# The context gate g2 moves into the expert loop, and the next mixer adds two accumulators

## The chip, the cores and the metric

The kernel runs on one core of a Trainium2 chip. The metric is the device time of one execution in microseconds (us). Before the change it was 2565.54 us, the median of three runs (2559.32 to 2566.08). The engines are TensorE (PE, matmuls; PEld is its weight load), VectorE (DVE), ScalarE (ACT), GpSimd (POOL) and the sync engine (SP), which only issues DMAs. All data are float32 unless a row says otherwise.

## The reference, cut to what matters

The program is a two-layer backbone over 512 latent tokens and 256 context tokens of width 1024. Layer 0 has a mixer of RG-LRU and differential attention and then a mixture of experts (MoE) over all 768 tokens. Layer 1 has an S5 mixer and then an MoE over the 512 latent tokens. The MoE routes each token to 6 of 64 experts (hidden width 256) and adds a shared expert; its result is multiplied by the modulation row g2 (g2c for context tokens) and added to x.

```python
def moe_ffn(h, ...):
    affinity = sigmoid(h @ router_w)
    _, idx = lax.top_k(affinity + router_bias, TOP_K)
    s_sel = take_along_axis(affinity, idx, -1)
    gates = s_sel / sum(s_sel) * ROUTED_SCALE
    ...                                   # tokens sorted by expert, in blocks
    def expert_block(acc, blk):
        tok, g, e = blk
        y = swiglu(h_ext[tok], w_gate[e], w_up[e], w_down[e])
        return acc.at[tok].add(y * g[:, None]), None
    ...
    return acc[:n_tok] + swiglu(h, ws_gate, ws_up, ws_down)

# layer 0
out = moe_ffn(concatenate([h2c, h2]), *moe_w)
ctx = ctx + g2c * out[:n_ctx_tok]
x = x + g2 * out[n_ctx_tok:]
# layer 1: the S5 mixer reads rms_norm(x) and rms_norm(ctx), then
x = x + g1 * y
x = x + g2 * moe_ffn(h2, *moe_w)
```

## The kernel before

`moe_blocks` (L681) runs once per layer. Ahead of its loop stand the norm, the router, the shared expert (TensorE L1360 into a PSUM bank, ScalarE L1054 into `ysh`, DMA L1056 by ScalarE's queue into the first accumulator in DRAM, `accs[0]`, tile by tile) and a table of items. An item is an expert with up to 128 tokens (wide) or up to 64 (narrow). This input has 34 wide and 38 narrow items in layer 0, and 16 wide and 50 narrow in layer 1.

The loop (`trips`, L815 to L825) walks a written order: in trip b each engine does its steps of wide item i, then of narrow item i, each step behind a branch that asks whether the item is there. So 34 trips of layer 0 and 16 of layer 1 have both items (paired trips), the others a narrow item alone. The order of one engine's steps is fixed; engines meet only at semaphores. In a trip,
- SP loads the next items' gate, up and down weights (1 MB each, L855 and L861) into a ring of two slots for wide items and three for narrow ones;
- GpSimd gathers the tokens of a later item (L946, L952) and scatters a result with add into DRAM: wide items into `accs[0]` (L963), narrow ones into `accs[1]` (L974, two rows of 512 per token);
- TensorE multiplies by gate and up (L1431 wide, L1442 narrow), transposes the hidden rows (L1471 narrow), multiplies by down (L1460 wide, L1481 narrow), and in between turns one-hot marks into token indices and gates (L1369) and transposes gathered tokens (L1376, L1382);
- VectorE does `gated_wide`, `gated_narrow`, `rest_wide` and `rest_narrow`. `rest_wide` reads off indices and gate of a later wide item (`tokens`, L1238 to L1246) and makes the marks of the one behind it (`mark_wide`, L1224). `rest_narrow` first copies the transposed hidden rows from PSUM (L1283), for which TensorE's L1481 waits, and then does the same for a narrow item (`mark_narrow`, L1231);
- ScalarE does the silu, the evictions of transposed tokens (L1014, L1018) and the eviction of the result, scaled by the gate: L1085 for a wide item, L1092 for a narrow one.

At the end SP loads the g2 rows (L902) and both accumulators (L905), VectorE adds the two, multiplies by g2 and adds x (L1296, L1298, L1300, 128x1024 each, per tile of 128 tokens), and SP stores x tile by tile (L909), in layer 0 to a DRAM buffer `x_mid`, in layer 1 to the output.

`s5_mixer` (L1934) follows layer 0. SP loads x_mid in four pieces of 96 partitions x 2048 (L2005) into `XS`. ScalarE squares each of its eight rows (L2082), VectorE waits for small vectors, prepares them and the state's powers (L2142 to L2162) and scales the rows (L2165). Later SP loads x a second time, in the layout of the residual, from x_mid (L2032), while GpSimd loads `Tb` (L2071) for TensorE (L2314).

## Time and profile before

| | |
|---|---|
| median of three runs | 2565.54 us |
| profiled execution: its own time, its span | 2561.44 us, 2559.7 us |
| TensorE busy, share of the span | 2148.3 us, 84% |
| VectorE busy | 908.9 us, 36% |
| ScalarE busy | 607.8 us, 24% |
| GpSimd busy | 453.5 us, 18% |
| DMA over the span | 672.72 MB, mean 263 GB/s |

The span is what the trace covers of the profiled execution. A row of a timeline gives start, duration, engine, line, operation, output<-inputs and shape, and in brackets the engine's idle time ahead of it with what ended it; "issue" there means that the profile shows nothing that was waited for. A row of a group gives total busy time, the mean of one in ns, and the idle time ahead of all of them. Layer 0's expert loop runs from about 711 to 1453 us, the S5 mixer from about 1492 to 1812, layer 1's loop from about 1897 to 2528.

### The profile page before, as it was taken

The numbers are of one execution on the slowest core, as the hardware profiler recorded it, in microseconds if no ns is written. First come the engines' busy times: TensorE is split into PE (matmuls) and PEld (weight loads), VectorE is DVE, ScalarE is ACT, GpSimd is POOL, SyncE is SP. The second block draws the span as 40 slices with busy tenths as digits, with TensorE's granted clock in tenths as the row PEclk, the third lists the DMA queues.
The fourth block names the chain that finished last, engine by engine and source line by source line (L and its number), as shares of the span: only waits on it lengthen the run. The fifth ranks groups of instructions, "written<-read, shape, count | busy, mean of one in ns | idle before, by whom it ended". The sixth has DMA issues, their size and how long they took to land. (4 is left out here: it accounts for less than half of the span.)

```text
span 2559.7 us, 39554 instructions
## 1 busy us (share of the span) xinstructions
PE 2148.3 (84%) x11733; PEld 1190.5 (47%) x11734; DVE 908.9 (36%) x2012; ACT 607.8 (24%) x1047; POOL 453.5 (18%) x423
## 2 busy tenths in 40 slices
PE   5889999896999999999999516489789999987873
PEld 3665445644444444444444315154444444444442
DVE  8854375824512121111111267922431111111113
ACT  3443243602122121121212113130222122211110
POOL 1000000002112222222222211200113222232321
PEclk8999999998999999999999858799899999999997
DMA  9971102005699999999998557960389999899995
GB/s 354 374 266 38 36 30 82 1 0 194 263 334 359 352 358 359 354 358 350 356 364 286 178 181 245 272 224 0 144 353 380 353 358 358 277 388 365 392 379 196
DMA packets 167668, 672.72 MB, mean 263 GB/s; under 512 B 37858, under 2 KB 40898, under 8 KB 123546
## 3 DMA queue, kind: packets, MB, share of 16 engines
q1 hardware_dynamic: 116650, 577.23, 58.8%
q0 software_dynamic: 38208, 69.04, 11.1%
q10 hardware_dynamic: 12720, 25.27, 2.6%
q8 instruction: 54, 0.88, 0.1%
q14 instruction: 36, 0.29, 0.0%
HBM read 622.28 MB, written 89.24 MB: 278 GB/s over the span
## 5 line engine op out<-in xcount | busy, mean ns | idle before, releaser
L1431 PE MATMUL banks_l<-slotw_l,xTw_l 128*128 128x512 f32 x800 | 357.9, 600 | 24.8 <-issue 24.8
L1442 PE MATMUL banks_l<-slotn_l,xTn_l 128*64 128x256 f32 x2816 | 326.5, 385 | 35.1 <-issue 35.1
L1442 PEld LDWEIGHTS banks_l<-slotn_l,xTn_l 128*64 128x64 f32 x2816 | 212.1, 138 | 180.9 <-issue 107.8
L1431 PEld LDWEIGHTS banks_l<-slotw_l,xTw_l 128*128 128x128 f32 x800 | 148.5, 191 | 236.1 <-issue 236.1
L1481 PE MATMUL banks_l<-slotn_l,late_l 128*64 128x512 f32 x704 | 189.9, 615 | 18.2 <-DVE late_l L1283 16.3
L1460 PE MATMUL banks_l<-slotw_l,late_l 128*128 128x512 f32 x400 | 191.8, 602 | 15.4 <-DVE late_l L1269 15.4
L946 POOL DMA_INDIRECT xgw_l<-moe_h,idxw_l x58 | 60.7, 1047 | 770.9 <-PE banks_l L1376 634.5
L974 POOL DMA_INDIRECT moe_acc<-late_l,idxn_l x88 | 141.1, 1603 | 200.8 <-DMA moe_acc<-late_l,idxn_l 183.4
L1266 DVE TENSOR_TENSOR late_l<-late_l,banks_l 128x256 f32<-128x256 f32 x50 | 21.1, 422 | 341.0 <-ACT late_l L1072 341.0
L1231 DVE TENSOR_TENSOR onehotn_l<-iota_slot_l,rank_l 128x512 bf16 (+1 forms) x98 | 79.3, 809 | 133.5 <-issue 133.5
L556 PE MATMUL ps_a<-W_a,hT_a 128*128 128x512 f32 x288 | 124.1, 592 | 0.0
L952 POOL DMA_INDIRECT xgn_l<-moe_h,idxn_l x96 | 102.0, 1063 | 89.3 <-DVE idxn_l L1243 56.2
L2359 PE MATMUL ps_s<-UV_s,ZU_s 128*128 128x512 f32 x256 | 110.1, 592 | 0.7 <-ACT ZU_s L2106 0.7
L1092 ACT ACTIVATE late_l<-banks_l,gslotn_l 128x512 f32<-128x512 f32 x88 | 60.5, 688 | 184.7 <-PE banks_l L1481 171.3
L916 POOL MEMSET ident_l<- 128x128 f32 x2 | 0.4, 205 | 583.5 <-POOLq L69 428.6
L1072 ACT ACTIVATE late_l<-banks_l 128x256 f32<-128x256 f32 x50 | 19.2, 384 | 350.1 <-PE banks_l L1431 340.9
L1460 PEld LDWEIGHTS banks_l<-slotw_l,late_l 128*128 128x128 f32 x400 | 68.5, 191 | 71.3 <-issue 71.3
L1014 ACT ACTIVATE xTw_l<-banks_l 128x512 f32<-128x512 f32 x108 | 64.5, 597 | 151.8 <-PE banks_l L1376 149.8
L1077 ACT ACTIVATE late_l<-banks_l 128x128 f32<-128x128 f32 x88 | 24.5, 278 | 310.1 <-PE banks_l L1442 306.0
L963 POOL DMA_INDIRECT moe_acc<-yw_l,idxw_l x50 | 79.5, 1589 | 97.1 <-ACT yw_l L1085 95.9
L556 PEld LDWEIGHTS ps_a<-W_a,hT_a 128*128 128x128 f32 x288 | 54.7, 190 | 67.7 <-issue 67.4
L510 PE MATMUL ps_a<-hT_a,W_a 128*128 128x512 f32 (+1 forms) x256 | 83.0, 486 | 1.0 <-ACT hT_a L195 1.0
(397 smaller groups left out, 3057.0 us busy)
## 6 DMA issues: line engine op xcount, KB each, us to landing
slotn_l<-in_exp_w_gate SPq DMA_DIRECT2D x88, 1024.0 KB
slotn_l<-in_exp_w_up SPq DMA_DIRECT2D x88, 1024.0 KB
slotn_l<-in_exp_w_down SPq DMA_DIRECT2D x88, 1024.0 KB
slotw_l<-in_exp_w_gate SPq DMA_DIRECT2D x50, 1024.0 KB
slotw_l<-in_exp_w_up SPq DMA_DIRECT2D x50, 1024.0 KB
slotw_l<-in_exp_w_down SPq DMA_DIRECT2D x50, 1024.0 KB
w_p<-in_mod_w SPq DMA_DIRECT2D x12, 2048.0 KB, 15.7
...
```

The costliest lines, as they stand in the source:

```text
L510: last = pe.matmul(bank(4 + 2 * (f % 2), b - a, a), W[:, c % 2, k, f * P:(f + 1) * P], hT[:, k, a:b], start=(k == 0), stop=(k == KD - 1))
L556: last = pe.matmul(bank(n % 4), hT[:, k, t * P:(t + 1) * P], W[:, c % 2, k, :], start=(k == 0), stop=(k == KD - 1))
L952: pool.indirect_dma_start(xg_n[b % 3][:], None, h_half, bass.IndirectOffsetOnAxis(idx[1][b][:].bitcast(U32), 0), bounds_check=last_half, o ...
L963: pool.indirect_dma_start(accs[0], bass.IndirectOffsetOnAxis(idx[0][b][:].bitcast(U32), 0), y_w[b % 2][:], None, bounds_check=last_row, oo ...
L974: pool.indirect_dma_start(acc_half, bass.IndirectOffsetOnAxis(idx[1][b][:].bitcast(U32), 0), y_n[b % 2], None, bounds_check=last_half, oob ...
L1014: act.activation(xT_w[b % 2][:, 4 * half:4 * half + 4, :], pT_w.rearrange("p (k c) -> p k c", c=P), ACT.Copy).then_inc(W['xT_done'], 1)
L1231: dve.tensor_tensor(onehot[1][:].rearrange("p t (a s) -> p t a s", a=2), where, rank[:, :, bass.ds(e, 1)].rearrange("p t (a o) -> p t a o" ...
L1431: last = pe.matmul(pGU_w, xT_w[b % 2][:, k, :], wgu[0][b % WIDE_RING][:, :, k, :], start=(k == 0), stop=(k == KD - 1))
L1442: last = pe.matmul(pGU_n[H * side:H * side + H, b % 2], xT_n[b % 2][:, k % 4, H * (k // 4):H * (k // 4) + H], w[:, :, k, P * side:P * side ...
L1460: last = pe.matmul(pY_w[:, half * 512:(half + 1) * 512], hidT_w[:, k, :], wd[0][b % WIDE_RING][:, k, half * 512:(half + 1) * 512], start=( ...
L1481: last = pe.matmul(pY_n[H * side:H * side + H, :], hidT_n[:, H * k:H * k + H], w[:, k, side * 512:(side + 1) * 512], start=(k == 0), stop= ...
L2359: last = pe.matmul(ps[:, (2 * (u % 4) + half) * 512:(2 * (u % 4) + half + 1) * 512], zT[:, k, m * P:(m + 1) * P], glu[n][:, k, half, :], s ...
```

## The change

The accumulators start otherwise. `accs[1]` gets x in place of zeros (SP, L858), and `accs[0]` gets the shared result multiplied by g2: VectorE's `start_row` (L1264) multiplies one tile of `ysh` into the buffer of x, and ScalarE's queue stores it (`store_start`, L1060). In the loop a result is multiplied by gate and g2 as it leaves PSUM, on VectorE and no longer on ScalarE (`result_wide`, L1324; the end of `rest_narrow`, L1332). In layer 0 an item can hold latent and context tokens, so g2 differs by row: for each item VectorE first makes the row's g2 in the result buffer as `g2_dif * late_row + g2_lat` (L1316 for a wide item), with `late_row` 1 or 0 per token (L1256). VectorE has six steps in a trip where it had four. The final multiply by g2 and add of x are gone. In layer 1 one add per tile is left; in layer 0 nothing is loaded or stored, and the S5 mixer loads both accumulators (L2066), adds them row by row (L2201) and copies the residual out of SBUF (L2077).

```diff
@@ SP, start of moe_blocks
+            for s in range(streams):
+                sp.dma_start(g2[:, s, :], mr[s:s + 1, 5 * D:6 * D].to_broadcast([P, D])).then_inc(R['g2_in'], 16)
             for t in range(NT):
-                sp.dma_start(accs[1][t * P:(t + 1) * P, :], zero).then_inc(R['zero_out'], 16)
+                sp.dma_start(accs[1][t * P:(t + 1) * P, :], x[:, t, :]).then_inc(R['x_kept'], 16)
@@ SP, end of moe_blocks: the g2 loads go; the acc loads and the stores stay only for the output
+            if 'x_out' in st:
                 for t in range(NT):
                     for k, dst in enumerate((acc, acc1)):
                         sp.dma_start(dst[:, t, :], accs[k][t * P:(t + 1) * P, :]).then_inc(acc_in[t], 16)
@@ ScalarE, shared expert, tile t
-                act.dma_start(accs[0][t * P:(t + 1) * P, :], ysh[t % 2][:]).then_inc(y_out[t % 2], 16)
+                if t:
+                    store_start(t - 1)          # waits for start_row(t - 1)
@@ ScalarE, rest_wide (rest_narrow alike)
-                act.wait_ge(W['y_mm'], i + 1 + WIDE_RING)
-                act.wait_ge(yw_added, i * 16 + 16)
-                act.activation(y_w[b % 2][:], pY_w, ACT.Copy, scale=gslot[0][b][:]).then_inc(W['y_done'], 1)
@@ VectorE, tokens
+                if streams > 1:
+                    dve.tensor_scalar(late_row[kind][b][:], idf[kind][:], float(LAT - BIG), None, ALU.is_ge)
@@ VectorE, ahead of the loop
+            def start_row(t):
+                s = 1 if t >= NT - ctx_tiles else 0
+                dve.wait_ge(R['sh_y_done'], 2 * t + 2)
+                dve.tensor_tensor(x[:, t, :], ysh[t % 2][:], g2[:, s, :], ALU.mult).then_inc(R['init'], 1)
@@ VectorE, the loop
                 mark_wide(i + (AHEAD + 1))
+                if streams > 1:
+                    dve.scalar_tensor_tensor(out=y_w[b % 2][:], in0=g2_dif, scalar=late_row[0][b][:], in1=g2_lat,
+                                             op0=ALU.mult, op1=ALU.add).then_inc(W['g_done'], 1)
-            def rest_narrow(i, q, b):
+            def turned_narrow(i, q, b):
                 dve.wait_ge(N['hidT_mm'], i + 1)
                 dve.wait_ge(N['y_mm'], i + NARROW_RING)
                 dve.tensor_copy(hidT_n, pHT[:, 0, :]).then_inc(N['hidT_done'], 1)
+            def result_wide(i, q, b):
+                dve.wait_ge(W['y_mm'], i + 1 + WIDE_RING)
+                dve.scalar_tensor_tensor(out=y_w[b % 2][:], in0=pY_w, scalar=gslot[0][b][:],
+                                         in1=y_w[b % 2][:] if streams > 1 else g2_lat,
+                                         op0=ALU.mult, op1=ALU.mult).then_inc(W['y_done'], 1)
+            def rest_narrow(i, q, b):
                 tokens(1, i + AHEAD, (b + AHEAD) % UNROLL)
                 mark_narrow(i + (AHEAD + 1))
+                ...                             # the g2 row of the item (layer 0), then its result, 128x512 each
@@ S5 mixer: SP, VectorE
+                for part, dst in zip(parts, (X, X1)):
+                    sp.dma_start(dst[:, 2 * j:2 * j + 2, :], part...[:, 2 * j:2 * j + 2, :]).then_inc(x_in[j], 16)
+            for s in range(SL):
+                dve.wait_ge(x_in[s // 2], 32)
+                dve.tensor_tensor(X[:, s, :], X[:, s, :], X1[:, s, :], ALU.add).then_inc(S['x_sum'], 1)
-                                 xin[0:LAT]...[2 * m + hh]).then_inc(S['xres_in'], 16)      # SP L2032
+                            sp.dma_start(x[hh * 64:hh * 64 + 64, m, :], X[0:64, 2 * m + hh, :]).then_inc(S['xres_in'], 16)
```

Smaller parts: 32 one-column memsets at the head of each MoE on VectorE; in layer 0 VectorE makes `g2_lat` and `g2_dif` once ahead of the loop, and SP's first narrow down load waits for it; in the S5 mixer, SP's and GpSimd's steps for the modulation bias wait for the copied residual.

How the rows of the program move is shown at three places. First VectorE in layer 0's loop, between the indices of a wide item and the narrow item's indices, in one trip. Before:

```order
L1224 ISA
L1224 TENSOR_TENSOR onehotw_l0<-iota_slot_l0,rank_l0 128x768
L821 UNCONDITIONAL_BRANCH
L821 COMPARE_AND_BRANCH
L1281 REGISTER_ALU
L1282 REGISTER_ALU
L1283 COPY late_l0<-banks_l0 128x128
L1284 ISA
L1237 REGISTER_ALU
L1238 TENSOR_REDUCE gslotn4_l0<-banks_l0 128x1
L1239 TENSOR_REDUCE idfn_l0<-banks_l0 128x1
```

After:

```order
L1237 TENSOR_TENSOR onehotw_l0<-iota_slot_l0,rank_l0 128x768
L1316 SCALAR_TENSOR_TENSOR yw0_l0<-x,lroww0_l0 128x1024
L828 UNCONDITIONAL_BRANCH
L828 COMPARE_AND_BRANCH
L1320 REGISTER_ALU
L1321 REGISTER_ALU
L1322 COPY late_l0<-banks_l0 128x128
L828 UNCONDITIONAL_BRANCH
L828 COMPARE_AND_BRANCH
L1325 REGISTER_ALU
L1327 REGISTER_ALU
L1328 SCALAR_TENSOR_TENSOR yw0_l0<-banks_l0,gslotw0_l0,yw0_l0 128x1024
```

Behind the mark (L1224, now L1237) stands the making of the g2 row (L1316), and only then the copy of the narrow item's hidden rows (L1283, now L1322); the wide result (L1328) follows it.

Second the sync engine, from the last weight load of layer 0 to the S5 mixer's small loads. Before (of the twelve L905 rows the last three):

```order
L905 DMA slotw1_l0<-moe_acc1 128x1024
L905 DMA slotw0_l0<-moe_acc0 128x1024
L905 DMA slotw1_l0<-moe_acc1 128x1024
L909 DMA x_mid<-x 128x1024 x6
L699 UNCONDITIONAL_BRANCH
L2002 UNCONDITIONAL_BRANCH
L2005 DMA XS_s<-x_mid 96x2048 x4
L2008 DMA vec_s<-modrow 64x2x16 x2
L2009 DMA vec_s<-in_norm1_g 64x16
L2010 DMA lam_s<-s5_l8 128x256
```

After:

```order
L699 UNCONDITIONAL_BRANCH
L2062 UNCONDITIONAL_BRANCH
L2066 DMA XS_s<-moe_acc0 96x2048
L2066 DMA ZU_s<-moe_acc1 96x2048
L2066 DMA XS_s<-moe_acc0 96x2048
L2066 DMA ZU_s<-moe_acc1 96x2048
L2066 DMA XS_s<-moe_acc0 96x2048
L2066 DMA ZU_s<-moe_acc1 96x2048
L2066 DMA XS_s<-moe_acc0 96x2048
L2066 DMA ZU_s<-moe_acc1 96x2048
L2069 DMA vec_s<-modrow 64x2x16 x2
L2070 DMA vec_s<-in_norm1_g 64x16
```

The loads of x_mid come right behind the loop as loads of both accumulators, to the mixer's own tiles; the loads, the stores and the g2 rows between are gone.

Third ScalarE at the head of layer 1's loop: L1054 (now L1073) evicts a tile of the shared expert, L1056 (now L1062) stores one, L1014 and L1018 (now L1029 and L1033) evict transposed tokens. Before:

```order
L1043 ACTIVATE late_l1<-banks_l1 128x256
L1054 ACTIVATE yw0_l1<-banks_l1 128x512 x2
L1056 DMA moe_acc0<-yw0_l1 128x1024
L1014 ACTIVATE xTw_l1<-banks_l1 128x512
L1054 ACTIVATE yw1_l1<-banks_l1 128x512 x2
L1056 DMA moe_acc0<-yw1_l1 128x1024
L1014 ACTIVATE xTw_l1<-banks_l1 128x512
L1018 ACTIVATE xTn_l1<-banks_l1 128x512
L1014 ACTIVATE xTw_l1<-banks_l1 128x512
```

After:

```order
L1073 ACTIVATE yw0_l1<-banks_l1 128x512 x2
L1062 DMA moe_acc0<-x 128x1024
L1029 ACTIVATE xTw_l1<-banks_l1 128x512
L1073 ACTIVATE yw1_l1<-banks_l1 128x512 x2
L1062 DMA moe_acc0<-x 128x1024
L1029 ACTIVATE xTw_l1<-banks_l1 128x512
L1033 ACTIVATE xTn_l1<-banks_l1 128x512
L1029 ACTIVATE xTw_l1<-banks_l1 128x512
L1062 DMA moe_acc0<-x 128x1024
```

A store now follows the eviction of the next tile, and the last one stands behind all evictions of tokens; each waits for VectorE's `start_row`.

## Rows read from the trace of the kernel before

**Rows 1.** stretches of both loops: busy PE, PEld, DVE, ACT, POOL, PEclk, DMA, GB/s
```profile
726.00:1400.00 674.00, 635.59 (x2964) 316.69 (x2964) 130.38 (x391) 135.39 (x228) 175.66 (x132) 1.00 0.97 352
2223.00:2463.00 240.00, 193.42 (x1318) 111.27 (x1314) 45.72 (x161) 41.93 (x81) 70.25 (x53) 0.99 1.01 377
```

**Rows 2.** the page's costliest groups, two of TensorE: busy, mean, idle before
```profile
L1431 PE MATMUL banks_l<-slotw_l,xTw_l 128*128 128x512 f32 x800 | 357.9, 600 | 24.8 <-issue 24.8
...
L1481 PE MATMUL banks_l<-slotn_l,late_l 128*64 128x512 f32 x704 | 189.9, 615 | 18.2 <-DVE late_l L1283 16.3
```

**Rows 3.** timeline, TensorE in a paired trip of layer 0
```profile
913.76 1.08 PE L1481 MATMUL banks_l<-slotn_l,late_l 128*64 128x512 f32 x4 [0.28 <-DVE late_l L1283]
...
916.93 7.13 PE L1431 MATMUL banks_l<-slotw_l,xTw_l 128*128 128x512 f32 x16 [0.36 <-issue]
```

**Rows 4.** timeline, VectorE in the same trip
```profile
912.55 0.96 DVE L1224 TENSOR_TENSOR onehotw_l<-iota_slot_l,rank_l 128x768 bf16 x1 [1.43 <-issue]
913.43 0.28 DVE L1283 COPY late_l<-banks_l 128x128 f32<-128x128 f32 x1
915.61 0.16 DVE L1238 TENSOR_REDUCE gslotn_l<-banks_l 128x1 f32<-128x3 f32 x1 [1.90 <-PE banks_l L1369]
...
917.67 0.96 DVE L1231 TENSOR_TENSOR onehotn_l<-iota_slot_l,rank_l 128x768 bf16 x1 [1.51 <-issue]
```

**Rows 5.** timeline, ScalarE in the same trip
```profile
913.02 1.11 ACT L1085 ACTIVATE yw_l<-banks_l,gslotw_l 128x1024 f32<-128x1024 f32 x1 [1.21 <-PE banks_l L1460]
```

**Rows 6.** groups by shape, two of VectorE: busy, mean ns
```profile
L1126 DVE SCALAR_TENSOR_TENSOR slotn_l<-x,ss_l,slotn_l 128x1024 f32<-128x1024 f32 x10 | 12.8, 1285 | 0.8 <-ACT ss_l L1025 0.5
...
L1246 DVE TENSOR_SCALAR idxw_l<-idfw_l 128x1 int32<-128x1 f32 x58 | 8.9, 154 | 6.2
```

**Rows 7.** VectorE at the head of layer 0's expert part
```profile
609.17 1.22 DVE L1110 SCALAR_TENSOR_TENSOR slotn_l<-slotn_l 128x1024 f32<-128x1024 f32 x1 [7.99 <-DMA slotn_l<-modrow]
610.31 2.40 DVE L1115 TENSOR_SCALAR ss_l<-ss_l 128x6 f32<-128x6 f32 x1
```

**Rows 8.** the sync engine's issues, layer 0's end to S5 mixer
```profile
1458.36 6.66 SPq L905 DMA_DIRECT2D slotw_l<-moe_acc  x12
1470.01 18.59 SPq L909 DMA_DIRECT2D x_mid<-x  x6
1492.35 0.80 SPq L2005 DMA_DIRECT2D XS_s<-x_mid  x2
```

**Rows 9.** stretches of the accumulator loads and of the x_mid loads
```profile
1468.00:1472.00 4.00, 0.00 (x0) 0.00 (x0) 3.93 (x4) 0.00 (x0) 0.00 (x0) 0.50 1.02 410
1500.00:1504.00 4.00, 0.00 (x0) 0.00 (x0) 0.00 (x0) 2.39 (x6) 0.00 (x0) 0.50 1.06 246
```

**Rows 10.** ScalarE at the last square that waits for a load
```profile
1508.41 1.06 ACT L2082 ACTIVATE UV_s<-XS_s 96x1024 f32<-96x1024 f32 x1 [0.99 <-DMA XS_s<-x_mid]
```

**Rows 11.** VectorE at the vector work and the scaling of x
```profile
1509.05 0.25 DVE L2142 SCALAR_TENSOR_TENSOR vec_s<-vec_s 64x16 f32<-64x16 f32 x2 [14.20 <-DMA vec_s<-in_norm_g]
...
1515.15 2.07 DVE L2165 TENSOR_SCALAR ZU_s<-XS_s,ss_s 96x1024 f32<-96x1024 f32 x3 [0.28 <-ACT ss_s L2085]
```

**Rows 12.** the sync engine's second load of x in the S5 mixer
```profile
1651.76 5.18 SPq L2032 DMA_DIRECT2D x<-x_mid  x8
```

**Rows 13.** TensorE behind it
```profile
1668.93 1.98 PE L2314 MATMUL ps_s<-Tb_s,UV_s 128*64 128x128 f32 x16 [12.71 <-DMA Tb_s<-s_kt]
```

**Rows 14.** ScalarE, the last expansion ahead of layer 1's loop
```profile
1896.58 0.60 ACT L1014 ACTIVATE xTw_l<-banks_l 128x512 f32<-128x512 f32 x1 [0.41 <-PE banks_l L1376]
```

**Rows 15.** VectorE in a paired trip of layer 1
```profile
2218.61 0.28 DVE L1283 COPY late_l<-banks_l 128x128 f32<-128x128 f32 x1
```

**Rows 16.** GpSimd in a narrow-only trip of layer 1
```profile
2391.33 1.59 POOL L974 DMA_INDIRECT moe_acc<-late_l,idxn_l  x1 [6.25 <-DMA moe_acc<-late_l,idxn_l]
```

**Rows 17.** VectorE and sync engine, end of the program
```profile
2539.89 1.23 DVE L1296 TENSOR_TENSOR slotw_l<-slotw_l 128x1024 f32<-128x1024 f32 x1 [12.94 <-DMA slotw_l<-moe_acc]
...
2543.67 12.07 SPq L909 DMA_DIRECT2D out<-x  x8
```

More of the change, by code:

```diff
@@ L768, in moe_blocks @@
         acc, acc1 = (slots[0][k][:, 0:NT * D].rearrange("p (t d) -> p t d", t=NT) for k in range(2))
-        g2 = slots[1][0][:, 0:streams * D].rearrange("p (s d) -> p s d", s=streams)
+        flat = x[:].rearrange("p t d -> p (t d)")
+        if streams > 1:
+            g2 = slots[1][0][:, GU:SLOT].rearrange("p (s d) -> p s d", s=streams)
+            g2_lat, g2_dif, g2_lat_n, g2_dif_n = carve(flat[:, 0:3 * D], (D, D, D // 2, D // 2))
+            late_row = [[sb(f"lrow{s}{b}", [P, 1]) for b in range(UNROLL)] for s in "wn"]
+        else:
+            g2_lat, g2_lat_n = carve(flat[:, NL * D:], (D, D // 2))
+            g2 = g2_lat.rearrange("p (s d) -> p s d", s=1)
         banks = ctx.enter_context(nc.psum_tensor(f"banks_l{layer}", [P, 8, 512], F32))
@@ L870, in _ @@
                 load_gate_up(kind, 0, 0)
-            for kind in range(2):
-                load_down(kind, 0, 0)
+            load_down(0, 0, 0)
+            if streams == 1:
+                load_down(1, 0, 0)
             load_gate_up(0, 1, 1)
@@ L996, in _ @@
             gather_narrow(3)
-            for b in range(2):
-                pool.wait_ge(y_out[b], 16 * (NT // 2))
-            pool.wait_ge(R['zero_out'], 16 * NT)
+            for t in range(NT):
+                pool.wait_ge(init_out[t], 16)
+            pool.wait_ge(R['x_kept'], 16 * NT)
             pool.wait_ge(R['tab_in'], 16)
@@ L1106, in _ @@
             dve.memset(row_base[64:P], 2.0 * BIG + 1.0).then_inc(R['consts'], 1)
+            for _ in range(32):
+                done(dve.memset(idf[0][:], 0.0))
+                done.wait()
             def gains(s):
@@ L1241, in tokens @@
                 dve.wait_ge(S[kind]['id_sum'], i + 1)
+                if streams > 1:
+                    dve.tensor_scalar(late_row[kind][b][:], idf[kind][:], float(LAT - BIG), None, ALU.is_ge)\
+                       .then_inc(S[kind]['row_in'], 1)
                 if kind:
@@ L1939, in s5_mixer @@
     x, cT = st['x'], st['cT']
-    xin = io['x_mid']
+    parts = st['moe_acc']
     ctx = ExitStack()
@@ L2012, in _ @@
                 if hb == 3:
+                    sp.wait_ge(S['x_sum'], SL)
+                    for m in range(NL):
+                        for hh in range(2):
+                            sp.dma_start(x[hh * 64:hh * 64 + 64, m, :], X[0:64, 2 * m + hh, :]).then_inc(S['xres_in'], 16)
                     sp.wait_ge(S['bias_zero'], 1)
```

127 lines of the change are left out of this document (74 added, 53 removed).

## Prediction

> **What bounds the kernel now.** I read the busy time by stretches first. In layer 0's expert loop TensorE is busy 635.59 of 674 us while the DMA engines stand at 0.97 [rows 1], so both are candidates. The page's groups separate them: nothing in the loop makes TensorE wait for a weight load. Its idle time stands before L1431, where no releaser is shown, and before L1481, where VectorE's copy L1283 ended 16.3 of 18.2 us [rows 2]. The stretch of layer 1's loop with narrow items alone reaches a DMA share of 1.01 at 377 GB/s, so the 352 GB/s of layer 0 is not the ceiling [rows 1]. I take TensorE's chain, with VectorE's copy in it, as what sets a paired trip of layer 0.
>
> Then the timeline of one such trip. TensorE starts the narrow down product at 913.76 after 0.28 us idle, released by VectorE L1283 [rows 3]. VectorE ran the mark L1224 from 912.55 for 0.96 us and the copy from 913.43, right behind it [rows 4]. So whatever VectorE does between mark and copy is added to TensorE's path at full length. Behind the copy VectorE is idle for 1.90 us, and 1.51 us before L1231 [rows 4].
>
> Outside the loops the bound is a chain of loads and small steps, and there I read when the last wait of each ends.
>
> **Layer 0, paired trips.** The change puts the g2 row (`scalar_tensor_tensor`, 128x1024, SBUF inputs, scalar from a pointer) and one `late_row` operation of one column ahead of the copy. L1126 is the same operation with a pointer, 1285 ns; the 1.22 us of L1110 at 609.17 let the next instruction start at 610.31, 1.14 later [rows 6, 7]. The column operation is of L1246's kind, 154 ns long [rows 6]; in this run such ones start about 0.08 apart, and the 1.43 us of idle issue before the mark [rows 4] can swallow it. Bounds per trip: 1.14 from below, 1.285 + 0.154 = 1.44 from above, with a little issue 1.47. I take 1.20 + 0.08 = 1.28, since the copy starts at the mark's end less some overlap. 34 trips: 34 x 1.28 = +43.5 us (38.8 to 50).
>
> The result itself leaves ScalarE (L1085, from 913.02 for 1.11 us [rows 5]) and comes behind the copy on VectorE: about 915.0 to 916.3. The narrow indices read at 915.61 would then be due at 916.9, since the product before them is 1.28 later too; 0.5 us is spare, and I price this at nothing. If the cover were gone, it is rival B. The narrow g2 row and result stand behind L1231, after which VectorE has nothing until the next trip's gating, some 6 us later. ScalarE's work gets lighter, and nobody waits for it there. In the last trip nothing hides them: the last scatter is +1.5 later.
>
> **Layer 0 to the S5 mixer.** Before: accumulator loads issued at 1458.36, stores until 1488.60 (1470.01 + 18.59), the x_mid loads from 1492.35 [rows 8], the fourth landed at 1508.41 [rows 10], VectorE's small-vector work from 1509.05, the scaling from 1515.15 [rows 11]. After: the mixer can start where the accumulator loads did, a step between blocks (1.3 us) behind the last scatter's landing at 1457.5, so 1458.8. Eight loads in place of four: the fourth landed 16.06 us after the first issue, and a load of 786 KB takes 3.2 us at the 246 GB/s of its stretch [rows 9]; so 1458.8 + 16.06 + 4 x 3.2 = 1487.7. Two adds of the last pair (1.22 us each, cut to 96 partitions, no shorter) end at 1490.1. The vector work from 1509.05 to 1515.15, 6.1 us, comes behind it on VectorE: 1496.2, 19.0 us earlier than 1515.15. Bounds: 410 GB/s, as the accumulators were read with 128 partitions [rows 9], would bring the end to about 1485, -30; a mixer start 5 us later (tiles of the loop, instruction code) and a slower pace while the accumulators are read in the other order give -12. I take -19, by the nearer row, the same 96-partition pattern.
>
> The trace's 96-partition loads move 246 GB/s and the 128-partition ones 410 [rows 9]. The Trainium skill, page "SBUF — State Buffer", section "Door 1: The DMA port swizzle (why [64,N] ≈ [32,N])", says that partitions 0 to 63 reach only 8 of the 16 ports, with about 218 GB/s as their limit. An estimate from that page: 64 of the 96 partitions sit behind those 8 ports, so 218 x 96 / 64 = 327 GB/s, and 6.3 MB in 19.2 us; by the row's 246 it is 25.6 us. The trace agrees in direction, not in size; by the page the sum would come out some 6 us lower. I go by the row.
>
> **The second load of x.** It stood at 1651.76, eight loads over 5.18 us of issue [rows 12], and TensorE's L2314 waited 12.71 us for `Tb`, loaded at the same time [rows 13]. The copies from SBUF run at another time, and 2 MB less lie in front of `Tb`: 2 MB at 377 GB/s [rows 1] would be 5.6 us. I take -5 (0 to -6): `Tb` lands no earlier than its own issue allows.
>
> **Heads.** Layer 0: the 32 memsets (about 4 us) fall into VectorE's wait of 7.99 us before L1110 [rows 7], nothing. ScalarE no longer waits for stores of `ysh`; TensorE waited 0.77 us for it: -0.8. Layer 1: `store_start(2)` stands on ScalarE ahead of the last token evictions and waits for a 1.2 us multiply behind the last mark. The last L1014 was at 1896.58, released by TensorE [rows 14]; it moves +1.5 (0 to +2.5), and the loop's first product with it.
>
> **Layer 1, the loop.** No g2 row there, so in a paired trip the copy L1283 stays right behind the mark [rows 15]. The result on VectorE comes ahead of the narrow indices: +0.5 in all (0 to +5). With narrow items alone GpSimd's scatter waited 6.25 us for the scatter before [rows 16], and a result that is 1.6 us later (behind a mark of 0.69 us) is not seen: 0.
>
> **End of layer 1.** Before, the first add at 2539.89 was followed by eleven more operations of 1.22 us, until 2554.6, while the stores were issued from 2543.67 [rows 17]; the span ends 5.1 us behind the last. After, one add per tile: VectorE follows the loads, whose last pair lands near 2547.7 (1 MB per tile at about 400 GB/s, 2.6 us each, from the first at 2539.9), so the last add ends at 2549.0 and the span at 2554.1, -5.5; the last result is 0.7 later: -4.8 (-8 to -4).
>
> **Sum.** -0.8 + 43.5 + 1.5 - 19.0 - 5 + 1.5 + 0.5 - 4.8 = +17.4, so 2561.4 + 17.4 = 2578.8 for an execution like the profiled one. That one lay 4.1 us under the median of the three; 2565.5 + 17.4 = 2582.9. I predict 2581, between the two. A measurement of this kernel tells about 0.3% (7.7 us) from no change.
>
> **Rivals.**
> A, the other side: layer 0's loop is paced by the weight loads, and VectorE's 1.28 us falls into time that TensorE would have waited anyway. For it: DMA share 0.97 [rows 1], and idle time before L1431 without a releaser [rows 2]. Against: L1481's wait names VectorE, no wait names a load. It decides where a trip's bytes take longer than TensorE plus 1.28 us, that is nearly everywhere or not at all. Then the 43.5 is gone: 2581 - 43.5 = 2537.5.
> B: the wide result ahead of the narrow indices, and one more branch per trip, make VectorE late in every paired trip of both layers. For it: the spare time is only 0.5 us, and the marks have 1.43 and 1.51 us of issue before them [rows 4]. Against: who needs the narrow indices is a gather that has half a trip. 0.5 us in 50 trips: +25, so 2606.
> C: the accumulators come at 410 GB/s, since `x_mid` was read while its last stores were still landing. The scaling comes 11 us earlier still: 2570, within 0.3%. For it: the rate of the same buffers in rows 9. Against: the pieces stay 96 partitions x 2048 as in the row at 246 GB/s, and only their source changes.
>
> **How the numbers follow.** Forecast 0.62, A 0.08, B 0.12, C 0.18. The range reaches from C's faster half (2562) to short of B (2600): the bounds of the paired trips (-5, +7), of the mixer's start (+7, -11), of `Tb` (+5) and of layer 1's loop (+5) fit in. The forecast alone would be 2572 to 2593. Faster by over 0.3% is A and the low end of C: 0.10. Within 0.3% (2558 to 2573): most of C and the low edge of the forecast, 0.18. Slower: 0.72.
>
> **What would show it.** In the profile after, of a paired trip of layer 0: the g2 row between mark and copy, and TensorE's wait before the narrow down product grown from 0.28 to about 1.5 us, in all to some 60 us with VectorE's copy as the releaser; TensorE's busy share of that loop down to about 0.89. If the wait has grown but the trip has not, A is right. If waits for the indices (L1369's product or the gathers) appear in the pairs of both layers, B. In the mixer the scaling of x should start about 39 us behind the last scatter's landing (1457.5 to 1496.2); at about 28 us C is right. I would be wrong altogether if layer 0's loop were longer by under 30 us, or if layer 1's narrow trips had got longer.

## The result: 2605.8 us, 1.7% slower, and the profile after

The changed kernel takes 2605.78 us (median of 4 runs, 2597.99 to 2608.42); the kernel before, 2562.43 us (median of 4, 2557.27 to 2566.08). The ratio is 1.0168, with a 95% interval of 1.0149 to 1.0187. The forecast was 2581 us in a range of 2562 to 2600: the direction held, the loss of 43.4 us was 2.5 times the 17.4 that I had summed. The profiled execution took 2608.42 us, its span is 2606.7 us, 47.0 us longer than before.

First the same landmarks in both traces. Each is the start of a row; the last column is how far "after" had fallen behind by then.

| landmark | before | after | behind by |
|---|---|---|---|
| first expert product of layer 0 | 710.53 | 716.20 | 5.7 |
| last paired trip's first product | 1391.59 | 1460.47 | 68.9 |
| last scatter of layer 0 | 1451.84 | 1522.42 | 70.6 |
| scaling of x in the S5 mixer | 1515.15 | 1569.61 | 54.5 |
| first instruction of layer 1's MoE (VectorE) | 1813.89 | 1863.05 | 49.2 |
| first expert product of layer 1 | 1899.34 | 1948.67 | 49.3 |
| last paired trip's first product | 2202.03 | 2251.74 | 49.7 |
| last scatter | 2527.14 | 2580.42 | 53.3 |
| end of the span | 2559.7 | 2606.7 | 47.0 |

Most of the loss is made in the 33 periods of layer 0's paired trips, from the first product of one trip to that of the next: 744.3 us in place of 681.1, so 63.2. Ahead of them stand 5.7, between them and the last scatter 1.7, and everything behind that scatter gives 23.6 back.

The stretch of that loop and the narrow-only stretch of layer 1, as in [rows 1]:

```profile
732.00:1470.00 738.00, 660.27 (x2979) 325.01 (x2980) 260.13 (x592) 80.03 (x163) 181.57 (x132) 0.97 0.91 322
2270.00:2510.00 240.00, 193.76 (x1312) 112.25 (x1311) 63.51 (x187) 22.73 (x52) 72.88 (x54) 0.99 1.00 370
```

TensorE is busy 660.27 of 738 us (0.895), the DMA share has fallen to 0.91, and the granted clock is 0.97 where it was 1.00. The layer 1 stretch reads for TensorE and the DMA engines nearly as before. The two TensorE groups of [rows 2] after:

```profile
L1490 PE MATMUL banks_l<-slotw_l,xTw_l 128*128 128x512 f32 x800 | 374.0, 622 | 25.4 <-issue 21.6
...
L1540 PE MATMUL banks_l<-slotn_l,late_l 128*64 128x512 f32 x704 | 199.2, 643 | 61.1 <-DVE late_l L1322 59.2
```

The wait before the narrow down product (L1540, was L1481) has grown from 18.2 to 61.1 us, 59.2 of it put down to VectorE's copy L1322. That is the forecast's row, within a microsecond (18.2 + 43.5 = 61.7). But two numbers ahead of the wait have changed too: the mean of one L1490 matmul is 622 ns where it was 600, and of one L1540 matmul 643 where it was 615. For 800 and 704 matmuls that is 16.1 and 9.3 us more busy time on the same work.

VectorE's timeline in one trip that shows it, answering to [rows 4]:

```profile
822.99 0.96 DVE L1237 TENSOR_TENSOR onehotw_l<-iota_slot_l,rank_l 128x768 bf16 x1 [1.79 <-issue]
823.87 1.28 DVE L1316 SCALAR_TENSOR_TENSOR yw_l<-x,lroww_l 128x1024 f32<-128x1024 f32 x1
825.07 0.28 DVE L1322 COPY late_l<-banks_l 128x128 f32<-128x128 f32 x1
```

Mark, g2 row, copy, as the order says; the row takes 1.28 us and the copy starts 1.20 behind the row's start. TensorE in the same trip, as in [rows 3]:

```profile
825.59 1.24 PE L1540 MATMUL banks_l<-slotn_l,late_l 128*64 128x512 f32 x4 [2.08 <-DVE late_l L1322]
826.76 0.66 PE L1428 MATMUL banks_l<-pick_rhs_l,onehotn_l 128*128 x6
827.35 1.98 PE L1540 MATMUL banks_l<-slotn_l,late_l 128*64 128x512 f32 x4
829.25 9.08 PE L1490 MATMUL banks_l<-slotw_l,xTw_l 128*128 128x512 f32 x16
```

It waited 2.08 us in place of 0.28. The four matmuls at 827.35 then take 1.98 us; before they took 1.08. The sixteen of L1490 take 9.08 us; before, 7.13. The granted clock (the third column from the right) of three stretches around it:

```profile
820.00:826.00 6.00, 3.92 (x23) 2.21 (x22) 3.45 (x8) 1.19 (x2) 1.04 (x1) 1.00 1.02 427
827.00:833.00 6.00, 6.00 (x13) 2.26 (x13) 2.87 (x7) 0.00 (x0) 2.91 (x3) 0.50 1.00 298
834.00:840.00 6.00, 6.00 (x27) 2.79 (x27) 0.42 (x1) 0.38 (x1) 0.31 (x1) 1.00 0.33 122
```

1.00 before and during the wait, 0.50 from 827 to 833, 1.00 again from 834: that is the lower of the two levels, 1.2 GHz for 2.4. Most trips wait and run their sixteen at full speed. The trip whose wait ended at 939.82, for instance, waited 1.55 us and took 7.13:

```profile
939.82 1.08 PE L1540 MATMUL banks_l<-slotn_l,late_l 128*64 128x512 f32 x4 [1.55 <-DVE late_l L1322]
...
943.05 7.13 PE L1490 MATMUL banks_l<-slotw_l,xTw_l 128*128 128x512 f32 x16 [0.42 <-issue]
```

In the whole loop 12 of the 34 L1490 groups took over 7.3 us, 15.5 us more than at 7.13 each. In the kernel before all 34 took 7.13 us, and the clock never left 1.00 between the first and the last of them. The trip shown has the longest wait of the loop, but length alone does not pick the trips. This one waited 1.53 us, less than the one at 939.82, and was slow:

```profile
1210.59 1.08 PE L1540 MATMUL banks_l<-slotn_l,late_l 128*64 128x512 f32 x4 [1.53 <-DVE late_l L1322]
...
1214.23 7.74 PE L1490 MATMUL banks_l<-slotw_l,xTw_l 128*128 128x512 f32 x16
```

The trace has 12 stretches at 0.50 in this loop. The first begins 0.9 us after TensorE has started the loop's first product. Each of the other eleven begins 0.8 to 2.2 us after TensorE has resumed work behind this wait. Eight last 3.4 us, four 6.8 us; the four long ones are those with sixteen matmuls of over 9 us.

The first product of the loop now waits for VectorE and runs at the low clock:

```profile
716.20 8.83 PE L1490 MATMUL banks_l<-slotw_l,xTw_l 128*128 128x512 f32 x16 [3.75 <-DVEq L1347]
```

At the boundary to the S5 mixer, GpSimd's last scatter, the sync engine's first load (as in [rows 8]), and VectorE's last adds, vector work and scaling (as in [rows 11]):

```profile
1522.42 1.59 POOL L989 DMA_INDIRECT moe_acc<-late_l,idxn_l  x1 [2.75 <-DVE late_l L1342]
```

```profile
1532.42 0.34 SPq L2066 DMA_DIRECT2D XS_s<-moe_acc  x1
```

```profile
1561.25 2.36 DVE L2201 TENSOR_TENSOR XS_s<-XS_s,ZU_s 96x1024 f32<-96x1024 f32 x2 [4.04 <-DMA ZU_s<-moe_acc]
1563.52 0.24 DVE L2204 SCALAR_TENSOR_TENSOR vec_s<-vec_s 64x16 f32<-64x16 f32 x2
...
1569.61 5.39 DVE L2228 TENSOR_SCALAR ZU_s<-XS_s,ss_s 96x1024 f32<-96x1024 f32 x8 [0.28 <-ACT ss_s L2144]
```

The eight loads take 1532.42 to 1561.25, 28.8 us. From 1540 to 1558 they move 240 GB/s, as the loads of [rows 9] moved 246. From last scatter to scaling it is 47.2 us, where it was 63.3. TensorE's wait for `Tb` ([rows 13]) is 8.19 us in place of 12.71:

```profile
1718.38 1.98 PE L2378 MATMUL ps_s<-Tb_s,UV_s 128*64 128x128 f32 x16 [8.19 <-DMA Tb_s<-s_kt]
```

And the end of the program, as in [rows 17]:

```profile
2591.18 1.22 DVE L1359 TENSOR_TENSOR slotw_l<-slotw_l 128x1024 f32<-128x1024 f32 x1 [11.76 <-DMA slotw_l<-moe_acc]
...
2600.29 1.23 DVE L1359 TENSOR_TENSOR slotw_l<-slotw_l 128x1024 f32<-128x1024 f32 x1 [1.93 <-DMA slotw_l<-moe_acc]
```

One add per tile follows the loads; 26.3 us from last scatter to the end of the span, where it was 32.6.

### The profile page after: what moved, and what is told of

Its sections match the earlier page's. It is cut to its first block and busy times, and to the rows that moved or that the text cites. A ratio compares the mean times of both kernels' runs of the same rounds, so it can differ in the third digit from the quotient of the medians.

```text
span 2606.7 us, 39891 instructions
## 1 busy us (share of the span) xinstructions
PE 2179.5 (84%) x11733; PEld 1204.8 (46%) x11734; DVE 1095.1 (42%) x2364; ACT 496.7 (19%) x909; POOL 463.8 (18%) x421
## 5 line engine op out<-in xcount | busy, mean ns | idle before, releaser
L1490 PE MATMUL banks_l<-slotw_l,xTw_l 128*128 128x512 f32 x800 | 374.0, 622 | 25.4 <-issue 21.6
L1490 PEld LDWEIGHTS banks_l<-slotw_l,xTw_l 128*128 128x128 f32 x800 | 155.0, 199 | 253.7 <-issue 249.1
L1540 PE MATMUL banks_l<-slotn_l,late_l 128*64 128x512 f32 x704 | 199.2, 643 | 61.1 <-DVE late_l L1322 59.2
L1519 PE MATMUL banks_l<-slotw_l,late_l 128*128 128x512 f32 x400 | 191.8, 602 | 15.5 <-DVE late_l L1305 15.5
L967 POOL DMA_INDIRECT xgn_l<-moe_h,idxn_l x96 | 115.0, 1198 | 76.7 <-DVE idxn_l L1259 49.8
L1091 ACT ACTIVATE late_l<-banks_l 128x256 f32<-128x256 f32 x50 | 19.2, 383 | 571.9 <-PE banks_l L1490 571.9
L1029 ACT ACTIVATE xTw_l<-banks_l 128x512 f32<-128x512 f32 x108 | 64.5, 597 | 153.3 <-PE banks_l L1435 148.7
L1305 DVE COPY late_l<-banks_l 128x256 f32<-128x256 f32 x50 | 21.2, 424 | 160.7 <-PE banks_l L1509 160.7
L1237 DVE TENSOR_TENSOR onehotw_l<-iota_slot_l,rank_l 128x768 bf16 (+1 forms) x60 | 51.9, 865 | 85.8 <-issue 85.8
```

The costliest lines, as they stand in the source:

```text
L967: pool.indirect_dma_start(xg_n[b % 3][:], None, h_half, bass.IndirectOffsetOnAxis(idx[1][b][:].bitcast(U32), 0), bounds_check=last_half, o ...
L1029: act.activation(xT_w[b % 2][:, 4 * half:4 * half + 4, :], pT_w.rearrange("p (k c) -> p k c", c=P), ACT.Copy).then_inc(W['xT_done'], 1)
L1490: last = pe.matmul(pGU_w, xT_w[b % 2][:, k, :], wgu[0][b % WIDE_RING][:, :, k, :], start=(k == 0), stop=(k == KD - 1))
L1519: last = pe.matmul(pY_w[:, half * 512:(half + 1) * 512], hidT_w[:, k, :], wd[0][b % WIDE_RING][:, k, half * 512:(half + 1) * 512], start=( ...
L1540: last = pe.matmul(pY_n[H * side:H * side + H, :], hidT_n[:, H * k:H * k + H], w[:, k, side * 512:(side + 1) * 512], start=(k == 0), stop= ...
```

## The experiments

After the result the open question was the 20 us by which 33 periods exceed 33 x 1.3. My theory 1: TensorE's longer wait costs its own length, and besides it makes the clock fall in some trips. The rival, theory 2: the low clock comes with what else the change does in the loop, above all VectorE's larger load (260.13 us busy in the 738 us stretch, 130.38 in 674 before). For each kernel the table gives the time, the 33 periods between the first products of the first and the last paired trip, the median wait before the narrow down product and the slow groups (L1490's sixteen matmuls over 7.3 us; the line has another number in some kernels). All but the first two columns are read from one profiled execution each.

| kernel | median us | ratio to before | 33 periods | median wait | slow of 34 |
|---|---|---|---|---|---|
| before | 2562.2 | 1 | 681.1 | 0.47 | 0 |
| after | 2605.8 | 1.0168 | 744.3 | 1.71 | 12 |
| row behind the copy | 2558.69 | 0.998 (0.9965 to 0.9995) | 701.0 | 0.51 | 2 |
| half of the row | 2571.5 | 1.0037 (1.0022 to 1.0053) | 714.4 | 1.16 | 6 |
| row twice | 2685.4 (one run) | | 823.2 | 3.01 | 33 |
| wait filled with matmuls | 2589.53 | 1.0108 (1.0076 to 1.0139) | 725.1 | 0.37 behind the filling | 0 |
| before, with the row alone | 2618.04 | 1.0205 (1.0182 to 1.0228) | 733.4 | 1.66 | 12 |
| row at the trip's head | 2547.09 | 0.9938 (0.9916 to 0.996) | 685.3 | 0.52 | 0 |
| the same, earlier release | 2543.78 | 0.9915 (0.9891 to 0.9939) | 685.1 | 0.51 | 0 |

### The row behind the copy

```diff
@@ rest_wide -> result_wide
-                if streams > 1:      # at the end of rest_wide
-                    dve.scalar_tensor_tensor(out=y_w[b % 2][:], in0=g2_dif, scalar=late_row[0][b][:], in1=g2_lat, ...)
             def result_wide(i, q, b):
+                if streams > 1:
+                    dve.scalar_tensor_tensor(out=y_w[b % 2][:], in0=g2_dif, scalar=late_row[0][b][:], in1=g2_lat, ...)
                 dve.wait_ge(W['y_mm'], i + 1 + WIDE_RING)
```

> Changed kernel with one move: in layer 0 the g2 row of a wide item is made behind the copy of the narrow hidden rows (at the head of result_wide), not between mark and copy. Same work on VectorE. Theory 1 (TensorE's longer wait in each paired trip costs its own length and also makes the clock fall in some trips): the wait before the narrow down product is back at 0.28 us, a paired trip at 20.4 to 20.7 us, the granted clock of the loop at 1.00; 34 x 1.29 = 44 us and 19 us of slow clock go, 2606 - 63 = 2543 us. Theory 2 (the clock falls because VectorE does more in the loop): the wait goes but the slow trips stay, 2606 - 44 = 2562 us. Rival B of the prediction (results on VectorE make the indices late): the trip stays above 21 us and the time above 2580.

Measured: 2558.69 us, 47 us below the changed kernel and not 63. The longer wait is gone, and the slow trips but for two, with all of the change's work still on VectorE: that is against theory 2. The two are the loop's first, behind 3.76 us of waiting, and one behind 1.26 us of idle time; the clock of the stretch 726 to 1400 rounds to 1.00. But the 33 periods are 20 us longer than before, and only 3.4 of them are the two slow trips' excess over 7.13 us. TensorE in one trip, then VectorE:

```profile
1051.62 1.08 PE L1540 MATMUL banks_l<-slotn_l,late_l 128*64 128x512 f32 x4 [0.35 <-DVE late_l L1319]
...
1055.37 7.13 PE L1490 MATMUL banks_l<-slotw_l,xTw_l 128*128 128x512 f32 x16 [0.95 <-DVE idxn_l L1259]
```

```profile
1051.28 0.28 DVE L1319 COPY late_l<-banks_l 128x128 f32<-128x128 f32 x1
1051.48 1.27 DVE L1323 SCALAR_TENSOR_TENSOR yw_l<-x,lroww_l 128x1024 f32<-128x1024 f32 x1
1052.79 1.28 DVE L1328 SCALAR_TENSOR_TENSOR yw_l<-banks_l,gslotw_l,yw_l 128x1024 f32<-128x1024 f32 x1
1053.99 0.15 DVE L1251 TENSOR_REDUCE gslotn_l<-banks_l 128x1 f32<-128x3 f32 x1
```

The product of the next trip waits 0.95 us for the narrow indices (L1259). Row and result stand behind the copy back to back, from 1051.48 to 1054.07, and the index work L1251 starts only with their end; in the kernel before it had 1.90 us to spare [rows 4]. TensorE waits for these indices at the end of its step. Its waits over the loop, and then the one at the same place in the kernel before (us in total, times, longest):

```profile
PE banks_l L1490 <- DVE idxn_l L1259: 21.5, 26, 1.0
PE banks_l L1540 <- DVE late_l L1319: 14.7, 31, 0.9
```

```profile
PE banks_l L1431 <- issue: 14.9, 33, 0.9
```

21.5 us in 26 trips end with the narrow indices; before, 14.9 us in 33 trips had no releaser, and none ended with the indices. That is the mechanism of rival B. In the changed kernel the spare time held, since only one of the two stands there.

### Half of the row

```diff
-                    dve.scalar_tensor_tensor(out=y_w[b % 2][:], in0=g2_dif, ...)                 # 1024 columns, ahead of the copy
+                    dve.scalar_tensor_tensor(out=y_w[b % 2][:, 0:512], in0=g2_dif[:, 0:512], ...)     # ahead of it
+                    dve.scalar_tensor_tensor(out=y_w[b % 2][:, 512:1024], in0=g2_dif[:, 512:1024], ...)  # behind it
```

> Changed kernel with the g2 row of a wide item cut in two: 512 columns between mark and copy, 512 behind the copy. The wait before the narrow down product should be about 0.28 + 0.65 = 0.93 us. By its own length that gives 34 x 0.62 = 21 us back: 2585. If the slow clock comes only behind waits of the longer kind, the 19 us go too: 2566. If any wait brings it in proportion: 2575.

Measured: 2571.5 us, median wait 1.16 us, six slow groups that add 6.2 us in all (one of them the loop's first, behind 3.76 us), and the clock of the stretch at 0.99:

```profile
726.00:1400.00 674.00, 614.19 (x2835) 304.25 (x2835) 254.16 (x597) 76.35 (x156) 167.06 (x125) 0.99 0.96 342
```

It lies between the sum without slow trips (2566) and the one in proportion to the wait (2575), a little nearer to the second. The shorter wait has fewer slow trips, not none, so I see no sharp length from which they come.

### The row twice

```diff
                     dve.scalar_tensor_tensor(out=y_w[b % 2][:], in0=g2_dif, ...).then_inc(W['g_done'], 1)
+                    dve.wait_ge(W['g_done'], 2 * i + 1)
+                    dve.scalar_tensor_tensor(out=y_w[b % 2][:], in0=g2_dif, ...).then_inc(W['g_done'], 1)
             ...                                       # result_wide waits for both
```

> Changed kernel with the g2 row of a wide item made twice in a row between mark and copy (the same values). The wait grows by another 1.3 us to about 2.85. Theory 1: own length 34 x 1.3 = 44 us more, and slow trips in more than the 17 of the changed kernel, 10 to 30 us more: 2660 to 2680. If the clock has nothing to do with the wait: 2650.

Measured: 2685.4 us in the one run, past the upper end of what theory 1 expected. (By the count used here the changed kernel has 12 slow trips and not the 17 named there.) One trip of TensorE:

```profile
1078.32 1.08 PE L1545 MATMUL banks_l<-slotn_l,late_l 128*64 128x512 f32 x4 [3.02 <-DVE late_l L1327]
...
1080.10 1.98 PE L1545 MATMUL banks_l<-slotn_l,late_l 128*64 128x512 f32 x4
1082.00 9.23 PE L1495 MATMUL banks_l<-slotw_l,xTw_l 128*128 128x512 f32 x16
```

The wait is 3.02 us. After it the second four matmuls run at half speed. The stretch of the loop:

```profile
730.00:1530.00 800.00, 693.85 (x2916) 329.18 (x2914) 294.33 (x609) 78.49 (x160) 169.07 (x128) 0.89 0.85 292
```

A clock of 0.89 on average; 33 of 34 groups are slow, by 41.9 us in these groups alone. The 33 periods are 142.1 us longer than before. An estimate: two rows of 44 each by their length, as in the next experiment, leave 54 for the clock.

### The wait filled with matmuls

```diff
             def rest_narrow(i, q, b):      # TensorE
+                pe.wait_ge(N['y_done'], i + 1)
+                if streams > 1:
+                    for _ in range(6):
+                        pe.matmul(pY_n[:, 0:P], ident[:], ident[:], start=True, stop=True)
                 pe.wait_ge(N['hidT_done'], i + 1)
```

The first added line only lets the engine write into that PSUM bank once the result before is out of it.

> Changed kernel in which TensorE, in layer 0, runs six products of 128x128 (identity by identity, into the bank that the next product overwrites) ahead of its wait for the copy; VectorE's work is the same. They take about 1.0 of the 1.25 added us, so the trip is not shorter by its waits. Theory 1 (idle time on TensorE lowers the clock): no trips at the low clock, 2606 - 19 = 2587 us, a paired trip at 21.7. Theory 2 (VectorE's load, or chance): slow trips as before, 2606.

Measured: 2589.53 us, no slow group at all, and the clock of the stretch:

```profile
726.00:1400.00 674.00, 638.16 (x3155) 338.35 (x3156) 241.79 (x550) 74.16 (x152) 169.22 (x123) 1.00 0.93 335
```

This is the experiment that separates the theories. VectorE does all that it does in the changed kernel, the copy is as late, and TensorE's useful work starts as late (33 periods of 725.1 us, a median of 21.92: 44.0 us over before, 1.33 a trip). Only the engine is not idle. The clock stays up, and 19.2 us of the 63.2 are gone. So the change's loss in the loop is 44.0 by the wait's length and 19.2 by the clock that falls behind it. The changed kernel's own trace gives the same split: the ten of its 33 periods in which the clock stayed at 1.00 are 1.32 us longer than before, 43.5 us for 33, and 19.7 are left. The medians of the whole kernels differ by less, 16.3 us.

### The kernel before with the row alone

```diff
@@ before, VectorE, rest_wide
                 mark_wide(i + (AHEAD + 1))
+                if streams > 1:
+                    dve.scalar_tensor_tensor(out=y_w[b % 2][:], in0=x[:, 0, :], scalar=gslot[0][b][:], in1=x[:, 1, :],
+                                             op0=ALU.mult, op1=ALU.add).then_inc(W['row_done'], 1)
@@ before, ScalarE, rest_wide
+                if streams > 1:
+                    act.wait_ge(W['row_done'], i + 1)
                 act.activation(y_w[b % 2][:], pY_w, ACT.Copy, scale=gslot[0][b][:]).then_inc(W['y_done'], 1)
```

> Kernel before with one addition: in layer 0 VectorE does one scalar_tensor_tensor of 128x1024 between mark and copy in each paired trip, into the result buffer, before ScalarE writes the result over it (ScalarE waits for it). Nothing else of the change is in it. Theory 1: the added wait alone makes both parts, 34 x 1.3 = 44 us by its length and about 17 us at the low clock, 2562 + 61 = 2623 us, with 10 to 15 slow trips. If the low clock needed the rest of the change (results on VectorE, less on ScalarE): 2606 us and no slow trips.

Measured: 2618.04 us, 55.6 us over before, with 12 slow groups. TensorE's wait for the copy, and the stretch:

```profile
L1486 PE MATMUL banks_l<-slotn_l,late_l 128*64 128x512 f32 x704 | 200.3, 646 | 59.0 <-DVE late_l L1288 57.2
```

```profile
726.00:1400.00 674.00, 604.89 (x2754) 298.71 (x2753) 158.08 (x396) 126.79 (x214) 161.17 (x122) 0.97 0.93 332
```

One instruction, put at that place (with ScalarE's wait for it) and nothing else, makes the wait (59.0 us) and the low clock (0.97). The 33 periods are 52.3 us longer. The ten of them in which the clock stayed at 1.00 are 1.20 us longer each, so 40 us are length and 12.6 the clock, less than in the changed kernel. The slow groups are shorter here (mostly 7.7 to 7.8 us, there up to 9.3), because all twelve stretches at 0.50 last 3.4 us and none 6.8. Why that is so I did not settle.

### The row at the head of the trip

```diff
             def gated_wide(i, q, b):
+                dve.wait_ge(yw_added, i * 16 + 16)
+                if streams > 1:
+                    dve.scalar_tensor_tensor(out=y_w[b % 2][:], in0=g2_dif, scalar=late_row[0][b][:], in1=g2_lat, ...)
                 dve.wait_ge(W['silu_done'], i + 1)
             def rest_wide(i, q, b):
-                dve.wait_ge(yw_added, i * 16 + 16)
                 tokens(0, i + AHEAD, (b + AHEAD) % UNROLL)
                 mark_wide(i + (AHEAD + 1))
-                if streams > 1:
-                    dve.scalar_tensor_tensor(out=y_w[b % 2][:], in0=g2_dif, scalar=late_row[0][b][:], in1=g2_lat, ...)
```

> Changed kernel with the g2 row of a wide item made at the head of the trip, ahead of gated_wide, where VectorE waits for the first product anyway; between mark and copy nothing, behind the copy only the result. Theory: the wait before the narrow down product is 0.28 us and the product behind the trip does not wait for the narrow indices (as it does, 0.95 us, where row and result both stand behind the copy), so a paired trip is back at 20.6 us as in the kernel before, without slow trips. Then the gains outside the loop are left: about 2562 + 1.6 (last item) - 16 (S5 start) - 5 (Tb) - 6 (end) + 2 (layer 1) = 2539 us. Rival: the result alone behind the copy already makes the indices late, 0.3 to 0.5 us a trip: 2550 to 2556.

Measured: 2547.09 us, ratio 0.9938 (0.9916 to 0.996): faster than the kernel before, some 8 us above what I expected. In the profile the expectation missed mostly two things: the 33 periods, 4.2 us longer than before, and layer 1, where the way to its first product is 3.2 us longer and the way from the last paired trip to the last scatter 5.3. One trip of TensorE, then of VectorE:

```profile
912.83 1.08 PE L1540 MATMUL banks_l<-slotn_l,late_l 128*64 128x512 f32 x4 [0.33 <-DVE late_l L1322]
...
916.05 7.13 PE L1490 MATMUL banks_l<-slotw_l,xTw_l 128*128 128x512 f32 x16 [0.42 <-issue]
```

```profile
912.49 0.28 DVE L1322 COPY late_l<-banks_l 128x128 f32<-128x128 f32 x1
912.69 1.27 DVE L1328 SCALAR_TENSOR_TENSOR yw_l<-banks_l,gslotw_l,yw_l 128x1024 f32<-128x1024 f32 x1
914.66 0.16 DVE L1251 TENSOR_REDUCE gslotn_l<-banks_l 128x1 f32<-128x3 f32 x1 [0.70 <-PE banks_l L1428]
...
918.97 1.28 DVE L1303 SCALAR_TENSOR_TENSOR yw_l<-x,lroww_l 128x1024 f32<-128x1024 f32 x1
```

The copy stands right behind the mark, the result behind the copy, and 0.70 us are left before the indices are due. The g2 row is made at 918.97, where VectorE waits for the first product of the next trip. The 33 periods are 685.3 us, 4.2 more than before (a median of 20.75 for 20.61). VectorE's chain has two more one-column operations of 0.07 us issue each, which would fit, but no run takes them out. Its stretch:

```profile
726.00:1400.00 674.00, 631.56 (x2941) 314.78 (x2938) 258.14 (x585) 78.45 (x160) 187.22 (x131) 1.00 0.98 351
```

DMA share 0.98 at 351 GB/s and a clock of 1.00, as in [rows 1]. The rival of this run, that the result alone makes the indices late, has fallen.

### The same, with an earlier release

```diff
+            for kind in range(2):
+                dve.sem_inc(S[kind]['hid_done'], 1)      # was behind the start rows and the g2 constants
             for t in range(AHEAD - (NT - PICKED), NT):
                 start_row(t)
```

> The row_at_head kernel, with VectorE's release of TensorE for the first expert products (sem_inc of hid_done) moved ahead of the last start rows and the g2 constants, in both layers. The first product of layer 0's loop waited 3.75 us for it; it should go, and the low clock of that first trip (8.83 in place of 7.13 us) may go with it: 4 to 6 us below row_at_head, 2534 us. If the wait only moves to the first gating on VectorE: no difference.

Measured: 2543.78 us (4 runs, 2535.62 to 2547.99) against 2547.09 (6 runs, 2538.13 to 2554.52) of the kernel without it. The ranges overlap, so by the times the step is unclear. The trace shows it at its place. The first product of layer 0's loop in the row_at_head kernel, and in this one:

```profile
708.37 7.13 PE L1490 MATMUL banks_l<-slotw_l,xTw_l 128*128 128x512 f32 x16 [3.75 <-DVEq L1347]
```

```profile
707.79 7.13 PE L1491 MATMUL banks_l<-slotw_l,xTw_l 128*128 128x512 f32 x16 [0.69 <-issue]
```

The wait falls from 3.75 to 0.69 us, and from VectorE's first instruction of the MoE to this product it is 105.6 us (602.23 to 707.79) where it was 108.6 (599.77 to 708.37): 3 us. The low clock that the expectation hoped to save at this place was not there to save: in the row_at_head kernel the first sixteen matmuls already took 7.13 us behind the same wait of 3.75 us that has 8.83 behind it in the changed kernel.

## Why the prediction was wrong, by its own steps

**What bounds layer 0's loop: right.** TensorE's chain with VectorE's copy in it, and not the weight loads. Rival A is out: where the wait before the narrow down product grew, the loop grew, and the DMA share gave way (0.97 before, 0.91 after, 0.85 with the row twice). The signs that I had named came: 61.1 us of waiting with VectorE's copy as the releaser, and TensorE busy 0.895 of the loop.

**The step that failed: layer 0's paired trips, "34 x 1.28 = +43.5 us (38.8 to 50)".** The price per trip was right: the g2 row's 1.28 us, copy 1.20 behind its start, waits from 18.2 to 61.1 us, and 44.0 us with the wait filled. What the term took for granted is that the rest of the trip costs what it cost before. It costs more, because TensorE's clock falls behind some of the waits: 19.2 us more in this loop. The term was 63, not 43.5, and its upper bound of 50 was too low, because all the bounds were durations of VectorE's instruction. The clock of 1.00 in [rows 1] said nothing of longer waits. TensorE's waits for VectorE there, in the kernel before (total, times, longest), all stayed short:

```profile
PE banks_l L1481 <- DVE late_l L1283: 13.6, 33, 0.5
PE banks_l L1460 <- DVE late_l L1269: 10.2, 33, 0.3
```

And an example of the low clock behind longer idle time stood in the same trace, the first product of layer 1's loop: 8.57 us for sixteen matmuls that take 7.13 elsewhere, behind 2.80 us of idle time.

```profile
1899.34 8.57 PE L1431 MATMUL banks_l<-slotw_l,xTw_l 128*128 128x512 f32 x16 [2.80 <-issue]
```

**The results on VectorE, priced at nothing: right for this order.** The 0.5 us of spare time held in the changed kernel, and 0.70 us are left in row_at_head. Rival B's mechanism is real, and it starts when another 1.3 us stands behind the copy. There it cost about 17 us in layer 0 alone (the 20.0 less the 3.4 of two slow trips), where I had given it 25 for both layers. Rival B's time, 2606, is what the changed kernel measured, but that is a coincidence: no wait of TensorE in that loop ends with the indices, and the 25 us over the forecast came mostly from the clock.

**The start of the S5 mixer, "-19 (-12 to -30)": -16.1.** The loads took 28.8 us, where 16.06 + 4 x 3.2 = 28.9 was the sum, so the 96-partition pace of [rows 9] carried over (240 GB/s), and rival C is out. The estimate worked out from the Trainium skill, page "SBUF — State Buffer", section "Door 1: The DMA port swizzle (why [64,N] ≈ [32,N])", was 19.2 us for these bytes; at the 240 GB/s measured they take 26.2, and with the way to the first landing 28.8. The measurement decides. The 3 us that are missing lie ahead: the first load comes 10.0 us behind the last scatter's start in all seven kernels with the change (1522.42 to 1532.42 here), where I had 5.65 + 1.3. The 5.65 are from the kernel before, its last scatter and the first load behind it:

```profile
1451.84 1.59 POOL L974 DMA_INDIRECT moe_acc<-late_l,idxn_l  x1 [0.30 <-issue]
```

```profile
1457.49 0.82 SPq L902 DMA_DIRECT2D slotn_l<-modrow  x2
```

What fills the 3 us I did not test.

**The second load of x, "-5": right.** From the scaling to the first instruction of layer 1's MoE it is 293.4 us, before 298.7: -5.3. The other kernels with the change take 291.5 to 296.6 us for this way, so the hit is good to some 3 us and no better.

**Heads, "-0.8" and "+1.5": the first is off.** Layer 0's first product fell 5.7 us behind, 1.5 of it ahead of the MoE. I had not priced what stands on VectorE between the last start row and the release of TensorE: a wait of 3.75 us, of which head_and_release saves 3. But that wait is not what makes this head long. From the MoE's first instruction to this product it is 113.7 us here and in the row_behind_copy kernel, and 108.5 to 108.6 us in the four others with the same head and the same wait (half_row, row_twice, filled_wait, row_at_head); before it was 109.5. What differs in the traces is how long the clock stays low at the start of the MoE: 30.7 us in the two long ones, 17.1 in the four short ones, 23.9 before. TensorE has work in nearly all of this stretch, at a clock of 0.56 here, 0.74 before and 0.98 in the row_at_head kernel (the first two shown):

```profile
617.00:634.00 17.00, 16.42 (x87) 16.05 (x86) 13.08 (x11) 5.04 (x9) 0.00 (x0) 0.56 0.73 285
```

```profile
617.00:634.00 17.00, 16.42 (x112) 16.05 (x112) 12.47 (x11) 6.40 (x12) 0.00 (x0) 0.74 0.71 284
```

So about 5 us of the head in this profile are the clock's, and since kernels with the same head differ by them, I can't call them the change's. Layer 1's head: +0.2 here, and 2.4 to 3.2 in all the other kernels, the one before with the row alone included.

**Layer 1's loop, "+0.5" and 0: +0.4 in the pairs, +3.6 in the rest.** The scatters still set the pace there: from 2270 to 2510 GpSimd's scatter waits for the one before it 25 times, 136.0 us in all, and from 2223 to 2463 in the kernel before 25 times, 143.3 us. In the other kernels with the change this way took 326 to 330 us, before 325.1, and 326.6 in the kernel before with the row alone; so one to three us of it may be the change's. Longer narrow trips in layer 1 were a sign that I had named for being wrong; I leave open whether it came.

**End of layer 1, "-4.8": -6.3.** The right mechanism. The first add comes 10.8 us behind the last scatter where it was 12.8, which I had not counted on, and the rest gained 4.3 in place of 5.5.

Summed by these: 5.7 + 63.2 + 1.7 - 16.1 - 5.3 + 0.1 + 0.4 + 3.6 - 6.3 = 47.0. Against the forecast's 17.4 the clock in the loop is 19, layer 0's head 6.5, the boundary and layer 1's scatters 3 each; layer 1's head and the end take 1.5 each off, and the rest is small.
